# Two transformer blocks on one core: a third bank for turned probabilities, one bank for both outputs, and new ends

## The reference

```
x = x + token_mixer(rms_norm(x))     # pooling mixer and sparse attention (compressed, selected, window), gated and merged
x = x + conv_ffn(rms_norm(x))        # 2 x 2752 wide, three-tap convolution, silu(gate) * val
x = x + hybrid_mixer(rmsnorm(x))     # neighbourhood attention and bidirectional gated linear attention
x = x + sqrelu_mlp(rmsnorm(x))       # 4096 wide
return rmsnorm(x)
```

## Time and profile before

| | |
|---|---|
| runs (us) | 3219.55, 3216.07, 3219.4; median 3219.4 |
| the profiled execution (us) | 3216.57 |
| its span (us), first to last instruction | 3214.8 |
| mean granted clock of TensorE | 0.988 of full speed |
| busy: PE, DVE, ACT, POOL (us) | 3101.8, 1476.5, 1200.7, 396.6 |
| the chain that ended last | PE 90%, ACT 4%, DVE 3%, issue 2%, POOL 1% |

### The profile page before, as it was taken

The page is one execution under the profiler, slowest core; times in us unless marked ns, Lnnn a source line. Parts: engine busy times, 40 slices in busy tenths (PEclk is TensorE's granted clock), DMA queues, the critical chain, the costliest instruction groups (busy, mean ns, idle before and its releaser), DMA issues.

```text
span 3214.8 us, 42841 instructions
## 1 busy us (share of the span) xinstructions
PE 3101.8 (96%) x16934; PEld 2536.8 (79%) x16934; DVE 1476.5 (46%) x2224; ACT 1200.7 (37%) x1836; POOL 396.6 (12%) x616
## 2 busy tenths in 40 slices
PE   8999998999999999999999999999999999999997
PEld 6888887787778878888888778557778788888886
DVE  6652357666653435524533532565454322222233
ACT  4651138877663233312212331465442311212121
POOL 0110007655542000000000000120010000000000
PEclk9999998999999999999999999999999999999999
DMA  3222320000004211111111131001102111111111
GB/s 139 83 79 75 110 80 8 2 1 2 1 1 152 90 46 48 50 46 52 46 46 52 46 129 46 21 2 33 40 14 98 46 46 52 46 51 47 46 52 65
DMA packets 49898, 168.02 MB, mean 52 GB/s; under 512 B 8816, under 2 KB 9968, under 8 KB 49376
## 3 DMA queue, kind: packets, MB, share of 16 engines
q1 hardware_dynamic: 38784, 125.96, 11.7%
q0 software_dynamic: 10976, 40.15, 3.5%
HBM read 143.54 MB, written 16.78 MB: 50 GB/s over the span
## 4 chain that ended last, share of the span: by engine, by line
PE 90%; ACT 4%; DVE 3%; issue 2%; POOL 1%; DMA 0%; DVEq 0%; ACTq 0%; SPq 0%; POOLq 0%
PE PS L226 70%; PE PS L859 3%; PE PS L845 3%; PE PS L241 3%; PE PS L830 2%; PE PS L829 2%; PE PS L1617 1%; PE PS L1644 1%; PE PS L1629 1%; ACT PT L938 1%; ACT P_SHORT L928 1%; PE PS L880 1%; DVE PT L1027 1%; PE PS L871 0%; PE PS L315 0%
## 5 line engine op out<-in xcount | busy, mean ns | idle before, releaser
L199 ACT CAST WHI<-RAW 128x1024 fp32r<-128x1024 f32 x219 | 230.3, 1052 | 1355.0 <-PE PS L226 1334.3
L204 DVE TENSOR_TENSOR WLO<-RAW,WHI 128x1024 fp32r<-128x1024 f32 x219 | 268.7, 1227 | 1001.9 <-ACT WHI L199 1001.6
L226 PE MATMUL PS<-HLO,WHI 128*128 128x512 f32 x2160 | 667.5, 390 | 0.0
L226 PEld LDWEIGHTS PS<-HLO,WHI 128*128 128x128 f32 x2160 | 406.9, 188 | 85.1
L226 PE MATMUL PS<-X_HI,WHI 128*128 128x512 f32 x1504 | 467.4, 392 | 4.5 <-DVE W L336 2.2
L226 PE MATMUL PS<-X_HI,WLO 128*128 128x512 f32 x1504 | 464.7, 390 | 0.0
L226 PEld LDWEIGHTS PS<-X_HI,WHI 128*128 128x128 f32 x1504 | 282.4, 189 | 66.9 <-DVE W L2137 2.6
L226 PEld LDWEIGHTS PS<-X_HI,WLO 128*128 128x128 f32 x1504 | 283.6, 189 | 59.4
L226 PE MATMUL PS<-HID_HI,WHI 128*128 128x512 f32 x864 | 266.7, 390 | 6.4 <-DVE HID_LO L1349 6.4
L226 PE MATMUL PS<-HID_HI,WLO 128*128 128x512 f32 x864 | 266.4, 390 | 0.0
L226 PE MATMUL PS<-HID_LO,WHI 128*128 128x512 f32 x864 | 266.4, 390 | 0.0
(11 more groups left out here) (334 smaller groups left out, 4548.8 us busy)
## 6 DMA issues: line engine op xcount, KB each, us to landing
RAW<-in_w SPq DMA_DIRECT2D x219, 512.0 KB, 3.3
X<-in_x SPq DMA_DIRECT2D x8, 512.0 KB, 7.8
Q<-QN POOLq DMA_DIRECT2D x32, 128.0 KB, 2.7
merged<-W POOLq DMA_DIRECT2D x8, 512.0 KB, 3.1
W<-gate POOLq DMA_DIRECT2D x8, 512.0 KB, 4.0
W<-merged POOLq DMA_DIRECT2D x8, 512.0 KB, 4.7
X<-in_x POOLq DMA_DIRECT2D x8, 512.0 KB, 10.7
x_kept<-X POOLq DMA_DIRECT2D x8, 512.0 KB, 7.6
```

The lines of the kernel that those rows point to most:

```text
L199: nc.scalar.copy(WHI[:, slot, :], RAW[:, slot, :]).then_inc(w_hi, 1)
L204: nc.vector.tensor_tensor(WLO[:, slot, :], RAW[:, slot, :], WHI[:, slot, :].bitcast(F32), ALU.subtract).then_inc(w_lo, 1)
L226: last = nc.tensor.matmul(o[:, half], w[:, slot, cols], x(k)[:, half], start=(k == 0 and w is WHI and x is hi), stop=(done and k == kcs - ...
```

## The change

In the first attention the turned banks become three (`c % 3`, waits for c - 3); the third lies where the second output had its bank. Both outputs move into one bank, 128 columns each, and `pe_cmp_values` of pair m waits until the output of pair m - 1 has been read by both engines. `act_out_hi` moves ahead of ScalarE's copies of the first batch, `dve_out_lo` ahead of the compressed sums and of the shift of the second head.

In the opening VectorE clears half a tile and TensorE multiplies it three times before it starts; `pe_first_units` waits for each operand just before its first use, at all three norms. In the first feed-forward the first two units after the last hidden tile both run over the ready tiles first. At the end the last two units are issued in three column pieces (512, 256, 256), with square, sum, mean, inverse root, scale and output DMA by piece, from a buffer `Y` of its own.

```diff
@@ -237,6 +237,13 @@
         def step(k, b):
             cols = slice(k * P, (k + 1) * P)
             for w, x in ((WHI, hi), (WHI, HLO), (WLO, hi)):
+                if x is HLO:
+                    pe.wait_ge(h_ready, 8 * n + k + 1)
+                elif w is WHI:
+                    pe.wait_ge(w_hi, u + b + 1)
+                    pe.wait_ge(hhi_done, 8 * n + k + 1)
+                else:
+                    pe.wait_ge(w_lo, u + b + 1)
                 for half in (slice(0, 512), slice(512, T)):
                     last = nc.tensor.matmul(PAIR[(j + b) % 2][:, half], w[:, (u + b) % 2, cols], x[:, k, half],
                                             start=(k == 0 and w is WHI and x is hi),
@@ -244,13 +251,10 @@
             if k == KC - 1:
                 last.then_inc(job_done, 1)
 
-        pe.wait_ge(w_lo, u + 1)
         if j:
             pe.wait_ge(evacuated, j - 1)
         for k in range(lead):
-            pe.wait_ge(h_ready, 8 * n + k + 1)
             step(k, 0)
-        pe.wait_ge(w_lo, u + 2)
         if j:
             pe.wait_ge(evacuated, j)
         for k in range(lead):
...
@@ -711,8 +714,8 @@
                                   fix("REP", [N_SLC]), fix("SBIAS", [N_SLC]))
     HMIN, HSUM, HINV = fix("HMIN", [8, 2]), fix("HSUM", [8, 2]), fix("HINV", [8, 2])
     assert at <= W_AT + 12 * KB
-    T_PS = [PS[:, 2 * T + 512 * i:2 * T + 512 * i + 512] for i in range(2)]
-    O_PS = [PS[:, 3 * T + 512 * i:3 * T + 512 * i + P] for i in range(2)]
+    T_PS = [PS[:, c:c + 512] for c in (2 * T, 2 * T + 512, 3 * T + 512)]
+    O_PS = [PS[:, 3 * T + P * i:3 * T + P * i + P] for i in range(2)]
     C0_PS = PS[:, 3 * T + 512:4 * T]
     s_done, shifted, exp_done, inv_done, p_done, t_done, pt_copied, pv_done, o_hi, o_free = (
         sem(n) for n in ("s_done", "shifted", "exp_done", "inv_done", "p_done", "t_done", "pt_copied", "pv_done",
...
@@ -834,15 +837,15 @@
 
         qt = qt_of(m)
         c = turned_at[m] + i
-        if c >= 2:
-            wait_copied(pe, c - 2)
+        if c >= 3:
...
-                last = nc.tensor.transpose(T_PS[c % 2][:, P * (2 * x + e):P * (2 * x + e) + P], src, IDENT[:, :])
+                last = nc.tensor.transpose(T_PS[c % 3][:, P * (2 * x + e):P * (2 * x + e) + P], src, IDENT[:, :])
         last.then_inc(t_done, 1)
 
     def pe_use(pe, m, batch):
...
@@ -864,8 +867,8 @@
     def pe_cmp_values(pe, m):
         s, pair = m // PAIRS, m % PAIRS
         wait_copied(pe, c_turned_at[s])
-        if m >= 2:
-            pe.wait_ge(o_free, m - 1)
+        if m:
+            pe.wait_ge(o_free, m)
...
@@ -983,14 +986,14 @@
                 act_queries_hi(act, next_seg(m, 0))
             if ahead and len(b) > 1:
                 act_exp(act, 2 * ahead, 0)
+            if m:
+                act_out_hi(act, m - 1)
             for i in b[0]:
                 act_copy(act, m, i)
             if ahead:
                 if len(b) == 1:
                     act_exp(act, 2 * ahead, 0)
                 act_exp(act, 2 * ahead, 1)
-            if m:
-                act_out_hi(act, m - 1)
             if ahead:
                 act_exp(act, 2 * ahead + 1, 0)
                 act_exp(act, 2 * ahead + 1, 1)
...
@@ -1154,6 +1157,8 @@
             if ahead:
                 dve_shift(dve, 2 * ahead, 0)
                 dve_shift(dve, 2 * ahead, 1)
+            if m:
+                dve_out_lo(dve, m - 1)
             if m in SUMMED:
                 dve_cmp_sum(dve, SUMMED[m])
             if m in SCORED:
@@ -1166,8 +1171,6 @@
                 dve_shift(dve, 2 * ahead + 1, 0)
                 dve_inverse(dve, 2 * ahead)
                 dve_shift(dve, 2 * ahead + 1, 1)
-            if m:
-                dve_out_lo(dve, m - 1)
             if len(b) > 1:
                 dve_copy(dve, m, b[1][0])
             if ahead:
...
@@ -1365,8 +1368,15 @@
                 pe_unit_at(pe, U_FF1_REST + b, 2 * p, hi_of(1), h_lo)
         pe_unit_at(pe, U_FF1_TAIL, 0, hi_of(1), h_lo)
         tile_ready = lambda k: pe.wait_ge(hid_lo, GROUP * FF1_FULL + k + 2)
-        for b in range(2):
-            pe_unit_at(pe, U_Z2 - KC + b, 0, hi, lo, FF1_REST, None if b else tile_ready)
+        for part in range(2):
+            for b in range(2):
+                u = U_Z2 - KC + b
+                j = jobs_before(u)
+                if not part:
+                    pe.wait_ge(w_lo, u + 1)
+                    pe.wait_ge(evacuated, j - 1)
+                product(pe, u % 2, j % 2, hi, lo, FF1_REST - 1 + part, 0, None if b else tile_ready,
+                        part * (FF1_REST - 1), part == 1)
         with pe.Fori(1, KC // 2) as t:
             for b in range(2):
                 pe_unit_at(pe, U_Z2 - KC + b, 2 * t, hi, lo, FF1_REST)
...
@@ -2165,7 +2175,28 @@
                 act_ff2_store(act, b, GROUP * g + GROUP + b, b)
         with act.Fori(0, GROUP // 2 - 1) as p:
             tiles(U_LAST_UP, 2 * p, GROUP * (FF2_GROUPS - 1) + 2 * p + 2, 2 * p + 2)
-        act_residual(act, U_LAST, 4, XB)
+        for t in range(KC - 2):
+            act_split(act, U_LAST + t + 2)
+            act.wait_ge(evacuated, jobs_before(U_LAST + t) + 1)
+            act_square(act, 4, t, XB[:, t, :])
+        for i, (a0, a1) in enumerate(END_COLS):
+            for b in range(2):
+                act.wait_ge(evacuated, J_END + 2 * i + b + 1)
+                if i == 0:
+                    act.wait_ge(acc_done, 7 * 4 + 5 + b)
+                nc.scalar.activation(SQ[b][:, a0:a1], XB[:, KC - 2 + b, a0:a1], ACT.Square).then_inc(sq_done, 1)
+            act.wait_ge(mean_done, 4 + i + 1)
+            nc.scalar.activation(LN_B[:, a0:a1], SIDE[0][:, a0:a1], ACT.Ln, bias=EPS_T[:, 0:1]).then_inc(ln_done, 1)
+            act.wait_ge(ln_done, 4 + i + 1)
+            nc.scalar.activation(RSTD[4][:, a0:a1], LN_B[:, a0:a1], ACT.Exp, scale=-0.5).then_inc(rstd_done, 1)
+
+    END_COLS = ((0, 512), (512, 768), (768, T))
+    J_END = jobs_before(UNITS - 2)
+
+    def end_sums(b, i):
+
...
@@ -2190,7 +2221,38 @@
                 dve_ff2_store(dve, b, GROUP * g + GROUP + b, b)
         with dve.Fori(0, GROUP // 2 - 1) as p:
             tiles(U_LAST_UP, 2 * p, GROUP * (FF2_GROUPS - 1) + 2 * p + 2, 2 * p + 2)
-        dve_residual(dve, U_LAST, 4, XB, lambda t: XB[:, t, :], lambda t: None)
+        for t in range(KC - 2):
+            if t:
+                dve_acc(dve, 4, t - 1)
+            dve_add_residual(dve, U_LAST + t, 0, XB, t)
+            dve_split(dve, U_LAST + t + 2)
+        dve_acc(dve, 4, KC - 3)
+        dve_end_add(dve, 0)
+        dve_end_add(dve, 1)
+        dve_end_scale(dve, 0)
+        dve_end_add(dve, 2)
+        dve_end_scale(dve, 1)
+        dve_end_scale(dve, 2)
+
+    def dve_end_add(dve, i):
+
+        a0, a1 = END_COLS[i]
+        for b in range(2):
+            x = XB[:, KC - 2 + b, a0:a1]
+            dve.wait_ge(job_done, J_END + 2 * i + b + 1)
+            nc.vector.tensor_tensor(x, x, end_sums(b, i), ALU.add).then_inc(evacuated, 1)
+        dve.wait_ge(acc_done, 7 * 4 + 6 + i)
+        dve.wait_ge(sq_done, 8 * 4 + 6 + 2 * i + 1)
+        nc.vector.tensor_tensor(ACC[:, a0:a1], ACC[:, a0:a1], SQ[0][:, a0:a1], ALU.add).then_inc(acc_done, 1)
+
+    def dve_end_scale(dve, i):
+
+        a0, a1 = END_COLS[i]
+        dve.wait_ge(rstd_done, 4 + i + 1)
+        dve.wait_ge(evacuated, J_END + 2 * i + 2)
+        for k in range(KC):
+            nc.vector.scalar_tensor_tensor(Y[:, k, a0:a1], XB[:, k, a0:a1], NORM_W[:, 4, k:k + 1],
+                                           RSTD[4][:, a0:a1], ALU.mult, ALU.mult).then_inc(y_done, 1)
 
     def pe_ff2(pe):
         hi, lo = (lambda k: HID2_HI[:, k, :]), (lambda k: HID2_LO[:, k, :])
@@ -2209,16 +2271,35 @@
         tile_ready = lambda k: pe.wait_ge(hid2_lo, GROUP * (FF2_GROUPS - 1) + k + 2)
         for b in range(2):
             pe_unit_at(pe, U_LAST + b, 0, hi, lo, ready=None if b else tile_ready)
-        with pe.Fori(1, KC // 2) as t:
+        with pe.Fori(1, KC // 2 - 1) as t:
             for b in range(2):
                 pe_unit_at(pe, U_LAST + b, 2 * t, hi, lo)
-
-    def dve_final(dve):
-
-        dve.wait_ge(rstd_done, 5)
-        for k in range(KC):
-            nc.vector.scalar_tensor_tensor(X[:, k, :], XB[:, k, :], NORM_W[:, 4, k:k + 1], RSTD[4][:, :],
-                                           ALU.mult, ALU.mult).then_inc(y_done, 1)
+        for i, (a0, a1) in enumerate(END_COLS):
+            for b in range(2):
+                if i == 0:
+                    pe.wait_ge(w_lo, UNITS - 1 + b)
+                    pe.wait_ge(evacuated, J_END - 1 + b)
+                for k in range(KC):
+                    if i and b == 0 and k == 4:
+                        pe_end_mean(pe, i - 1)
+                    cols = slice(k * P, (k + 1) * P)
+                    for w, x in ((WHI, hi), (WHI, lo), (WLO, hi)):
+                        last = nc.tensor.matmul(end_sums(b, i), w[:, (UNITS - 2 + b) % 2, cols], x(k)[:, a0:a1],
```

(53 more changed lines are left out.)

5 lines of the change are left out of this document (2 added, 3 removed).

## The result

The changed kernel takes 3190.5 us (median of 4 runs, 3190.32 to 3191.7) against 3217.74 us of the kernel before (4 runs, 3215.16 to 3219.55): ratio 0.9916, 95% interval 0.9901 to 0.9931. It is faster by 27 us, where 55.7 were forecast. The profiled execution took 3190.32 us, with a span of 3188.5 and a mean granted clock of 0.987 (before: 0.988).

What follows compares the result with a forecast made beforehand. TensorE, busy 3101.8 of 3214.8 us, was taken as the bound, so only its stalls or lower clock could pay. Attention 40 + feed-forward 7.0 + opening 2.1 + tail 6.6 = 55.7 us, forecast 3162 us, range 3149 to 3189.

Steps and rivals of the forecast that it cites:

- The outputs in one bank, read at once: Attention: value matmuls wait for the outputs of pair m - 1, hidden by about 2 us of slack at tile 7.
- the tile 7 case: Attention, tile 7: ScalarE reads outputs before copying, so its 7 waits at the banks (4.0 us) stay.
- Rival 4: Attention: one output bank makes it slower, 63 pairs losing 1 us each past the slack, 3223 or more; chance 0.03.
- rival 1: Attention: ScalarE is the bound, a third bank only moves the wait; only VectorE's 13.9 us go, 3188; chance 0.17.
- The third bank in the long pairs: Attention, tiles 4 to 7: VectorE's copy waits go, ScalarE's stay at tile 7; a tile 5 pair 1.05 us shorter.
- The turn from short to long pairs: Attention: `dve_out_lo` now stands ahead of the compressed sums; 0.5 us of loss, once.
- Tiles 2 and 3 taken whole: Attention: bank waits of 2 to 3 us in each of four segments counted whole, 8 us, bounded below by half.
- the 40: Whole attention: 13.9 + 27.7 - 0.5 = 41, 1 off for ScalarE at tiles 2 and 3; between 27 and 48 us.
- The feed-forward: First feed-forward's last hidden tile: second unit's steps fill TensorE's 6.43 us wait; gain 7.0 us, bounds 5.0 and 7.5.
- The opening: Opening: dummy matmuls and finer waits let the mean start at 26.4 instead of 28.5; gain 2.1 us.
- the prediction's case of a falling clock: Opening: if the clock falls again between 7 and 9 us, TensorE is there at 27.6 and 0.9 us is left.
- The tail: After the last product: column pieces bring the end to 3208.2 from 3214.8; gain 6.6 us, bounds 4 and 9.

Runs made afterwards that it cites:

- reads_moved: The kernel before with only `act_out_hi` and `dve_out_lo` moved as in the change, two banks each: 3238.5 us, ratio 1.0072.
- one_bank_own_pair: The changed kernel with each short pair's outputs read at the end of its own iteration: 3166.8 us, ratio 0.9846 to the kernel before.
- p_ff1: The kernel before with only the split of the first output pair of the first feed-forward: ratio 0.9983, gain 5.5 us.
- p_opening: The kernel before with only the opening's edits (per-operand waits, three matmuls on zeros): ratio 0.9995, gain 1.6 us.
- p_tail: The kernel before with only the tail's edits (last output pair in three column blocks, results written in pieces): ratio 0.9984, gain 5.1 us.
- two_t_banks: The changed kernel with two banks for turned probabilities instead of three, outputs still in one bank, reads still ahead: 3240.3 us, ratio 1.0072 to the kernel before.
- p_attention: The kernel before with only the attention part of the change: 3208.5 us, ratio 0.9977.

## Why the prediction was wrong

**The step that failed** is in "The outputs in one bank, read at once": "In short tiles they also stand behind `pt_copied` of the same pair, which ScalarE makes after the reads", and from it "the price is nothing but the tile 7 case". The copy that follows the reads covers ScalarE's part of the chain alone. VectorE's part comes 0.59 us later, and later still by what is queued ahead of it, and the reads themselves delay the copy. The slack of 2 us was read at tile 7 and carried to tiles where a pair takes 3.6 to 6.9 us in place of 10.8 and ScalarE has little idle time. There the one bank costs 9.7 us and the moved reads 8.2 (6.1 in reads_moved), where the prediction had nothing for either; the third bank gives 1 us back. Rival 4 named this mechanism, but with 1 us for every pair; it came for half of the pairs, at 0.56 us each (16.7 over 30 pairs), and stayed inside the long ones' slack. That the time (3190.5) lies next to rival 1's 3188 is luck: rival 1 has ScalarE's waits at the banks stay, and they fell from 56 to 11.

The other steps:
- *The third bank in the long pairs.* Right in mechanism: no wait for VectorE's copies is left, and ScalarE's remain at tile 7 (7 waits, 3.6 us, 690 to 990 us, where the earlier trace rows has 2.4 between 913 and 993). Between marks 11 and 13 eight pairs take 70.0 us instead of 78.8: 1.10 us a pair, where 1.05 was forecast. The stretch as a whole gained 26.6 us, and 30.6 in one_bank_own_pair.
- *The turn from short to long pairs (0.5 us of loss).* It stands between marks 9 and 10: 37.3 us against 35.1 before (36.6 or 36.7 in p_ff1, p_opening and p_tail), 33.1 with the reads in their own pair. TensorE waits 2.5 us for the low parts there.
- *Tiles 2 and 3 taken whole (8 us).* Mis-sized. two_t_banks puts the third bank's worth in all the short pairs at 1 us beside the new wait; with that wait gone the short pairs are 2.4 us shorter than before in all. ScalarE's share was the warning. With 2.4 and 30.6 us, the attention of one_bank_own_pair gains 33 of the 40.
- *The feed-forward (7.0).* Right: 6.6 us at the boundary, in the changed kernel's trace and in p_ff1's. The wait for the third unit's weights was in the sum. Some 0.2 us is a misreading: the third unit of before starts at 1839.18, and 1839.38 is VectorE taking over the second unit's sum. By the medians of p_ff1 it is 5.5 within 3 either way.
- *The opening (2.1).* 0.8 us in the trace, 1.6 within 3 either way alone. The mean at 27.58 is where the prediction's case of a falling clock has it (27.6), and the clock did fall, but that is in part luck: VectorE's work began 1.0 us later than before (7.37 against 6.38), and its last sum ended at 27.19, so the mean could not have started at 26.4 at any clock. ScalarE saw the norm's weights land 1.8 us later in this trace (4.96 against 3.19). Whether the edit causes that is open: p_tail, with the old opening, has VectorE as late (7.44).
- *The tail (6.6).* 7.2 us in the trace (from the last stage's start to the end: 696.5 before, 689.3 after), 5.1 in the kernel of its own. The end is as worked out: 10.9 us behind the last product for a forecast 11.8, and 3.6 us more of TensorE for a forecast 3.3.
- *The sum.* VectorE splits 219 weight units in each kernel, and the same split in both traces tells how far ahead the changed kernel is: 0.8 us behind the opening, 10.6 behind the attention, 9.0 before the feed-forward's boundary, 15.6 behind it, 19.1 before the last stage, 26.3 at the end. So the four places give 0.8 + 9.8 + 6.6 + 7.2 = 24.4, and two stretches that were forecast at nothing give -1.6 (between 1198 and 1218 us) and +3.5 (in the second block, nearly all between 2285 and 2356 us). They go with the granted clock (third number from the end), before first:

```profile
2270.00:2350.00 80.00, 73.58 (x389) 61.26 (x389) 34.39 (x36) 21.92 (x21) 9.02 (x23) 0.91 0.10 33
```

```profile
2254.00:2334.00 80.00, 73.58 (x404) 61.88 (x403) 34.68 (x36) 21.93 (x21) 9.00 (x23) 0.96 0.10 33
```

In 1175 to 1215 us it is 1.00 before and 0.96 in the changed kernel. p_attention and p_tail, whose code there is that of before, have the same 1.6 us of loss, also at 0.96, and reads_moved, with the code of before, gains 1.6 and 1.5 us between 2322 and 2421. So single steps of about 1.6 us between two traces needn't come from an edit. Whether the whole is worth more than its parts (27 against 19.6 us) isn't known: by their intervals the difference isn't clear of noise.

The Trainium skill, *PSUM — Partial Sum Buffer*, section "PSUM bank collisions raise a hardware error", asks that two engines be kept out of one bank by a guard. The prediction took the guard's wait for the whole price, and put it at nothing. The wait is 27.0 us of idle time in the changed kernel and 0.7 once the reads of the short pairs were placed well. It isn't the whole: the reads that were moved for its sake cost besides. No run here shows a collision.

## What to carry to other kernels

When two users come to share a buffer, follow the release through every queue that it passes, in the shortest stage and not in the one with the most slack: at each engine, list what is ahead of the releasing instruction. If the release runs through two engines, look for the place where both reads follow their data at once without delaying the copies, as here at the end of the pair's own iteration; in the short pairs the same sharing cost 91 us at one place of the reads (282.4 against 191.1) and showed no cost at another (188.7). Test a reorder alone as well: here it cost 17 us in the long pairs, which the third bank's 44 would have hidden.

## What the runs showed of the hardware

Where TensorE waits more, its granted clock is lower too, but here this is the smaller part of the cost. These are the short pairs of the kernel before (first line) and of the changed one (second fence), from mark 0 to mark 9, the same 1469 matmuls (PE's busy time stands behind the length, the granted clock third from the end):

```profile
459.46:650.55 191.09, 171.54 (x1469) 145.07 (x1468) 134.56 (x497) 154.93 (x425) 126.53 (x176) 0.93 0.04 12
```

```profile
458.67:666.50 207.83, 174.43 (x1469) 153.08 (x1468) 136.39 (x498) 155.62 (x426) 126.42 (x176) 0.89 0.03 11
```

Of the 16.7 us, 13.8 are idle time of TensorE and 2.9 are more busy time, at a granted clock of 0.89 in place of 0.93. The clock doesn't follow the output bank's waits alone: one_bank_own_pair, where they are gone and the part is shortest (188.7), has 0.91.

The matmuls on zeros, from 1.47 to 6.82 us at the opening, were followed by one fast pair at 8.77 us (0.70); from 10.00 on, after 1.95 and 0.53 us of idle time, TensorE ran at 1.2 GHz again (1.22 and 1.06 a pair). In the kernel before, without them, the first pair at 9.13 took 1.19.
